# Cached rope keys turned on VectorE and moved by DMA; the last stage without GpSimd

## The reference

```python
# 8 sequences x 4 new tokens, 8 heads; 64 pages of 128 keys each
def mla_scores(q_lat, q_rope, c_kv, k_rope):        # latent part 256 wide, rope part 64 wide
    s = (einsum('bqhc,bkc->bhqk', q_lat, c_kv) + einsum('bqhr,bkr->bhqk', q_rope, k_rope))
    return s * ATTN_SCALE
...
def step(carry, pages):                              # running maximum, sum and accumulator
    m, l, acc = carry
    ck = cache_ckv[pages]
    kr = cache_krope[pages]
    s = mla_scores(q_lat, q_rope, ck, kr)
    m_new = jnp.maximum(m, jnp.max(s, axis=-1))
    alpha = jnp.exp(m - m_new)
    p = jnp.exp(s - m_new[..., None])
    l = l * alpha + jnp.sum(p, axis=-1)
    acc = acc * alpha[..., None] + einsum('bhqk,bkc->bhqc', p, ck)
    return (m_new, l, acc), None
...
out = ys[pos] * w_sorted                             # two expert rows of a token, by its gates
x = x + sum of the two
y = rmsnorm(x, norm_f_g)
```

## Time and profile before

| | us |
|---|---|
| median of 3 runs | 2081.01 (2080.91 to 2081.49) |
| the profiled execution | 2080.76 |
| its span, first to last instruction | 2078.8 |
| TensorE busy | 1874.1 (90%) |
| VectorE busy | 601.1 (29%) |
| ScalarE busy | 447.6 (22%) |
| GpSimd busy | 282.7 (14%) |
| mean granted TensorE clock | 0.948 |

### The profile page before, as it was taken

The page is one execution under the profiler, slowest core; times in us unless marked ns, Lnnn a source line. Parts: engine busy times, 40 slices in busy tenths (PEclk is TensorE's granted clock), DMA queues, the critical chain, the costliest instruction groups (busy, mean ns, idle before and its releaser), DMA issues. The chain is left out here.

```text
span 2078.8 us, 27133 instructions
## 1 busy us (share of the span) xinstructions
PE 1874.1 (90%) x10842; PEld 1112.7 (54%) x10842; DVE 601.1 (29%) x1358; ACT 447.6 (22%) x938; POOL 282.7 (14%) x424
## 2 busy tenths in 40 slices
PE   7999999999999999988999997999598988888870
PEld 5644444444455656756666664565355555555540
DVE  3110000000003334334555555466322211111116
ACT  3211111100012333232344442222110110110113
POOL 1021111000000000002222220122311111111101
PEclk9999999999999999998999998999698998999985
DMA  8212220222110000006777775444599999999966
GB/s 240 90 71 72 78 72 31 78 77 79 60 48 1 1 1 1 1 0 251 266 282 273 276 279 208 157 182 158 186 399 419 419 417 413 418 402 399 399 247 250
DMA packets 91425, 400.28 MB, mean 193 GB/s; under 512 B 22656, under 2 KB 28256, under 8 KB 60544
## 3 DMA queue, kind: packets, MB, share of 16 engines
q1 hardware_dynamic: 71040, 297.50, 36.6%
q0 software_dynamic: 20160, 101.24, 12.9%
q10 hardware_dynamic: 128, 0.20, 0.0%
HBM read 372.44 MB, written 46.88 MB: 202 GB/s over the span
## 5 line engine op out<-in xcount | busy, mean ns | idle before, releaser
L790 PE MATMUL psum<-arena 128*128 128x512 f32 (+1 forms) x1280 | 527.4, 567 | 0.0
L790 PEld LDWEIGHTS psum<-arena 128*128 128x128 f32 x1280 | 239.6, 190 | 259.8 <-issue 235.8
L1219 PE MATMUL psum<-arena 128*64 128x256 f32 (+1 forms) x2048 | 287.3, 415 | 65.5 <-DMA arena<-in_w_up_dram 65.1
L1219 PEld LDWEIGHTS psum<-arena 128*64 128x64 f32 (+1 forms) x2048 | 204.3, 156 | 138.7 <-issue 84.7
L1831 DVE COPY arena<-psum 128x512 f32<-128x512 f32 (+5 forms) x52 | 27.8, 544 | 522.4 <-PE psum L858 228.1
L1002 PEld LDWEIGHTS psum<-arena 128*128 128x128 f32 x1280 | 142.4, 142 | 29.3 <-issue 26.0
L1002 PE MATMUL psum<-arena 128*128 128x128 f32 x1280 | 154.1, 277 | 2.4 <-DVEq L1879 2.4
L1238 PE MATMUL psum<-arena 128*64 128x512 f32 (+1 forms) x512 | 131.3, 595 | 0.7 <-DVE arena L2145 0.7
L1376 ACT ACTIVATE arena<-psum 128x512 f32<-128x512 f32 (+1 forms) x72 | 40.5, 562 | 411.5 <-PE psum L790 400.7
L1393 ACT COPY arena<-psum 128x512 f32<-128x512 f32 x160 | 90.5, 587 | 176.8 <-PE psum L1002 176.8
L1887 DVE COPY arena<-psum 128x512 f32<-128x512 f32 x160 | 109.8, 691 | 36.6 <-PE psum L1002 34.0
(11 more groups left out here) (296 smaller groups left out, 1925.3 us busy)
## 6 DMA issues: line engine op xcount, KB each, us to landing
arena<-in_w_gate_dram SPq DMA_DIRECT2D x64, 1024.0 KB
arena<-in_w_up_dram SPq DMA_DIRECT2D x64, 1024.0 KB
arena<-in_w_down_dram SPq DMA_DIRECT2D x64, 1024.0 KB, 21.8
arena<-in_w_in_dram SPq DMA_DIRECT2D x8, 2048.0 KB, 7.9
z_act<-arena SPq DMA_DIRECT2D x64, 256.0 KB
arena<-z_act SPq DMA_DIRECT2D x8, 2048.0 KB, 9.7
arena<-in_x_prompt_dram SPq DMA_DIRECT2D x16, 512.0 KB, 4.7
arena<-y_rows SPq DMA_DIRECT2D x8, 1024.0 KB, 9.9
```

Source lines behind the costliest of these rows:

```text
L790: last = mm(out[:, 0:w], xn_t[:, k, t * P:t * P + P], w_blk[n % 2][:, k, 0:w], start=(k == 0), stop=(k == KD - 1))
L1219: last = mm(bank(2 + u)[rows, DE * x:DE * x + DE], xg_t[u][:, k, rows], w_e[slot][x][:, k, :], start=(k == 0), stop=(k == KD - 1))
```

## The change

**Rope part of the cache.** TensorE's units become the eight of the latent part; they use four banks (`u % 4`), and both copying engines have four copies. The rope part goes another way. `rope_blocks` on VectorE turns `kr[q]` in 32x32 blocks, one instruction for each half of the 64 features, into `kr_b[0]` and `kr_b[1]` (128 partitions x 512). After it, partition 32a+f of `kr_b[c]` holds feature 32c+f of the 512 keys in partitions 32a to 32a+31. `rope_move` on SP then issues eight transfers of 32 partitions x 2 KB that put these side by side as 64 partitions x 2048 keys, in one of the two halves of `kr_t2`. `score` reads it by a stepped view: pieces of 32 values.

There is one `kr_b`. `rope_blocks(n+2)` stands in round n of VectorE after its copies and before its sum update, and waits until the moves of chunk n+1 have landed (`rk_in`). The moves of n+2 wait for the blocks (`rk_t`) and for the scores of n (`c_s`). The scores of n+1 wait for the moves of n+1. `x_again(0)`, whose buffer now overlaps `kr_t2`, is issued after the stage's end, ahead of `w_o`.

**Last stage.** Tiles 2, 4 and 6 (`PE_TILES`) are summed by TensorE: `x2` times the identity, plus each expert row times a diagonal of gates (`diag`, made by VectorE), in PSUM; ScalarE and VectorE read the sum there. VectorE scales all nine tiles, two tiles behind the sums. ScalarE's scaling and GpSimd's multiplication are gone.

```diff
         def turned_at(u):
-            kind, j, c = turn_units[u]
-            return ck_t[:, c, j, :] if kind == "c" else kr_tt[:, j, :]
+            j, c = turn_units[u]
+            return ck_t[:, c, j, :]
...
+        def row_sum(t):
+            if t in PE_TILES:
+                return bank(2 * PE_TILES.index(t), 2)
+            return fin[t][0:rows_of(t), :]
...
+            def rope_move(s):
+                for c in range(2):
+                    for a in range(4):
+                        sp.dma_start(kr_t2[DR * s + 32 * c:DR * s + 32 * c + 32, 512 * a:512 * a + 512],
+                                     kr_b[c][32 * a:32 * a + 32, :]).then_inc(rk_in[s], 16)
+
+            for n in range(NCH):
+                sp.wait_ge(rk_t, n + 1)
+                if n >= 2:
+                    sp.wait_ge(c_s, n - 1)
+                rope_move(n % 2)
             for t in range(2):
                 sp.wait_ge(c_pv, NCH - 3 + t)
                 z_load(t)
-            x_again(0)
...
             sp.dma_start(g2, norm2_g[0].partition_broadcast(P)).then_inc(uv_in, 16)
+            x_again(0)
             sp.dma_start(w_o_sb, w_o[0].rearrange("(k p) n -> p k n", p=P)).then_inc(wo_in, 16)
...
-            def score(n):
+            def score(n, s, use):
+                half = slice(DR * s, DR * s + DR)
+                rope = kr_t2[half, :].rearrange("p (a r k) -> p r a k", a=4, r=PG)
                 for e in range(2):
-                    pe.wait_ge(kt_in[e], 5 * n + 5)
+                    pe.wait_ge(kt_in[e], 4 * n + 4)
+                pe.wait_ge(rk_in[s], use)
                 for c in range(3):
                     for j in range(4):
-                        half = slice(DR * (j % 2), DR * (j % 2) + DR)
+                        first = key_row(j, 0)
                         last = mm(bank(5)[RS * j:RS * j + RS, :], q_now[:, c, :] if c < 2 else qr_now[half, :],
-                                  ck_t[:, c, j, :] if c < 2 else kr_tt[half, j // 2, :], start=(c == 0), stop=(c == 2))
+                                  ck_t[:, c, j, :] if c < 2 else rope[:, first:first + 7:2], start=(c == 0), stop=(c == 2))
...
+            pe.wait_ge(moe_end, 1)
+            pe.wait_ge(r_dve, NT + 3)
+            for k, t in enumerate(PE_TILES):
+                pe.wait_ge(f_in[t % 4], 16 * (t // 4 + 1))
+                for half in range(2):
+                    cols = slice(512 * half, 512 * half + 512)
+                    mm(bank(2 * k + half), ident, x2[:, t, cols], start=True, stop=False)
+                    mm(bank(2 * k + half), diag[t][0], y2[t][:, cols], start=False, stop=False)
+                    last = mm(bank(2 * k + half), diag[t][1], y2[t][:, D + 512 * half:D + 512 * half + 512], start=False, stop=True)
+                last.then_inc(r_pe, 1)
...
-            def scale_odd(n):
-                act.wait_ge(f_inv, n + 1)
-                A(fin[n][0:rows_of(n), :], fin[n][0:rows_of(n), :], ACT.Copy, scale=stat8[n][0:rows_of(n), 1:2]).then_inc(f_sc, 1)
-
...
-            for t in range(1, NT, 2):
-                pool.wait_ge(f_sc, t // 2 + 1)
-                G.tensor_tensor(fin[t], fin[t], gf, ALU.mult).then_inc(f_okp, 1)
...
+            def rope_blocks(q, arrived, moved=None):
+                dve.wait_ge(c_in[q % 4], arrived)
+                if moved is not None:
+                    dve.wait_ge(rk_in[(q + 1) % 2], moved)
+                for c in range(2):
+                    last = V.transpose(kr_b[c].rearrange("p (r k) -> p r k", r=PG), kr[q % 4][:, :, 32 * c:32 * c + 32])
+                last.then_inc(rk_t, 1)
+
+            rope_blocks(0, 32)
             turned(0, range(1, NU, 2))
+            rope_blocks(1, 32, P)
...
                     if more:
                         turned(n + 1, range(1, NU, 2))
+                    if q < 2 or not last_batch:
+                        rope_blocks(q + 2, 32 * i + 32 * ((q + 2) // 4 + 1), 2 * P * i + P * ((q + 1) // 2 + 1))
                     dve.wait_ge(c_p, n + 1)
...
+            dve.wait_ge(moe_end, 1)
+            for t in PE_TILES:
+                for c in range(2):
+                    last = ts(diag[t][c], ident, gates[:, t, c:c + 1], None, ALU.mult)
+            last.then_inc(r_dve, 1)
...
             for t in range(NT):
                 r = rows_of(t)
-                dve.wait_ge(f_in[t % 4], 16 * (t // 4 + 1))
-                step(stt(fin[t][0:r, :], y2[t][0:r, 0:D], gates[0:r, t, 0:1], x2[0:r, t, :], ALU.mult, ALU.add))
-                stt(fin[t][0:r, :], y2[t][0:r, D:2 * D], gates[0:r, t, 1:2], fin[t][0:r, :], ALU.mult, ALU.add).then_inc(f_sum, 1)
-                if t >= 1:
-                    last_scale(t - 1)
+                if t not in PE_TILES:
+                    dve.wait_ge(f_in[t % 4], 16 * (t // 4 + 1))
+                    step(stt(fin[t][0:r, :], y2[t][0:r, 0:D], gates[0:r, t, 0:1], x2[0:r, t, :], ALU.mult, ALU.add))
+                    stt(fin[t][0:r, :], y2[t][0:r, D:2 * D], gates[0:r, t, 1:2], fin[t][0:r, :], ALU.mult, ALU.add).then_inc(f_sum, 1)
+                if t >= 2:
+                    last_scale(t - 2)
+            last_scale(NT - 2)
             last_scale(NT - 1)
```

77 lines of the change are left out of this document (36 added, 41 removed).

## The result

| | before | after |
|---|---|---|
| median of 4 runs, us | 2080.96 (2075.41 to 2081.49) | 2157.86 (2150.04 to 2163.55) |
| ratio to before | | 1.0373 (95%: 1.0333 to 1.0413) |
| the profiled execution, us | 2080.76 | 2163.55 |
| its mean granted TensorE clock | 0.948 | 0.934 |

A forecast was written before the change was run, and what follows sets the result against it. The prediction took TensorE to bound the cache stage before the change, and rope moves delayed by the gather after it: 2080.8 + 6.1 (start) - 0.9 (first round) + 17.1 (other rounds) - 10.3 (last stage) = 2093 us, range 2041 to 2108.

The forecast's parts named there:

- The chain: Cache stage: weighing releases the next gather, which delays the next moves and so the scores; round 10.1 us, +17.1 us.
- L: Cache stage: the time when a chunk's rope keys land; the next was put at L-d+11.6 us.
- d: Cache stage: how long TensorE's scores wait for the rope keys to land; forecast 1.5 us a round.
- They end when gather and moves are through: Cache stage: the moves lie inside the gather and land after 6.7 us of gather, 1.3 of moves, 0.5 of signal.
- The turn between queues: DMA engines, cache stage: gather and move packets alternate one against one, so moves last about as long as a gather's 16 packets.
- the first rival: Cache stage: moves hidden, landing at 6.5 us, loop 8.0 us under TensorE's 8.63; total 2044 us, chance 0.30 (2040 to 2060).
- the first round: Cache stage: its first round still has free engines and takes 8.63 us, -0.9 us.
- Issues: SP's queue, cache stage: eight transfers issue in 3.41 us, 0.43 each; in quiet the last lands 5.1 us after the first issue.
- The third: Rival, cache stage: transfers start 2 us later under load or transposes take 1.38; 15 us per us; 2108, no separate chance.
- The start: Start of the cache stage: first moves join four queued gathers and land at 975.8 us; +6.1 us, bounds 0 and +6.1.
- The last stage: Last stage: TensorE sums three tiles and VectorE ends at 2061.8 instead of GpSimd at 2072.16; -10.3 us, bounds -5 and -11.3.

The follow-up runs named there:

- e_fill: The changed kernel with 20 useless TensorE transposes a round before the scores' wait for the rope keys: 2148.6 us, ratio to before 1.0350.
- e_gather8k: The changed kernel with each latent gather of 16 KB rows issued as two gathers of 8 KB rows, same bytes: 2164.6 us, ratio to before 1.0420.
- e_queues: The changed kernel with four of a chunk's eight moves issued on ScalarE's queue instead of SP's: 2156.7 us, ratio to before 1.0390.
- e_two_first: The changed kernel with two pairs of block buffers, block transposes moved to the round's end, rope rows gathered before latent rows: 2129.2 us, ratio to before 1.0252.
- e_nogather: The changed kernel with the gathers inside the loop over sequences cut to 16 bytes a row: 2048.2 us, ratio to before 0.9864.

## Why the prediction was wrong

**The chain was right, one term of it was too small.** The prediction had L' = L - d + 3.1 + X, with X = 8.5 from the gather's reaching the engines to the landing (6.7 of gather, 1.3 of moves, 0.5 of signal), and a round of 8.63 + d. In the trace, the weighing starts at 1087.57 and 1096.75, so L - d is 1089.3 and 1098.5, and the landings are 1103.54 and 1113.53: X = 11.1 and 11.9. With X = 11.5 the same two equations give d = 3.0 and a round of 11.6 us; e_fill, whose clock stays up, has 11.73. The failed step is the size of X, the sentence "They end when gather and moves are through" with its 6.7 + 1.3 + 0.5 us. In the long rounds the sentence itself holds, and its terms are too small: the engines are full for 10.7 us instead of 8.0, some 7.7 of this gather where 6.7 stood, 2.0 of the moves where 1.3 stood, and 1.0 of the gather after, which had begun before the moves were through. In the short rounds the moves do not share the engines with the gather's 16 KB rows at all: they are served behind them, in 4.4 us where 1.3 stood. From the last packet to the landing it is 0.9 and 0.7 us; no row had shown the 0.5. That is 46 us of the miss (31 x 1.5).

**The turn between queues was half right.** From the earlier trace rows I took "one against one, whatever their size". Where both queues are served it is so, 46 packets beside 42 in the changed kernel and 95 beside 86 in e_gather8k. What the prediction did not have is the stretch before, in which queued moves are not served at all: 3.4 us and 67 rows of 16 KB in the long round shown, 3.0 us and 105 rows of 8 KB in e_gather8k, 1.6 us one pair of rounds later (1116.5 to 1118.1), and in the short round shown until the gather's rows are through. What decides between these is open. The Trainium skill, "DMA: Bandwidth & Descriptors", section on queues, rings and completion order, says that an engine changes rings only behind a whole packet, and that such a packet has 9 to 17 descriptors as a rule. The prediction took its packet for a record of the trace. Turns of 9 to 17 records are not what the trace shows where both queues are served: there the 47 records of moves stand singly between the gather's. A row packet's length, on which the first rival rested (cut to 4096 bytes, the moves would be hidden), brought no gain in either run that cut it.

**The clock was no term of the sum.** I priced a wait of TensorE at its length. One of 5 us also costs up to 2.5 us in what follows (scores busy for 5.38 us instead of 2.9 in 1127 to 1133.5). The busy time grew by 41 us; part of it replaced idle time. What it costs net is, by the profiled executions, the 0.5 us a round of e_fill, 12.24 - 11.73, 31 x 0.5 = 16 us. By the medians' ratios it is 0.0023 of 2081, 5 us, with overlapping intervals, so this term is the least certain one. The last 5 us of the rounds' miss are 4 that e_fill stands above 11.6 and 1.5 of the first round, which was not shorter. The warning was in the earlier trace rows, granted clock 0.77 in the stretch ahead of the rounds, which has a short wait, against 1.00 in them; I used the low level for the last stage alone.

**Issues.** Eight took 5.1 us, not 3.4, and without a gather the last packet starts 6.2 us after the first issue, where 5.1 stood for the landing; e_queues shows that in the real queue this cost next to nothing.

**The rivals.** The first (moves hidden, 2044 us) stood on 8.0 us of DMA time a round. The moves alone take 2.1 of it, not 1.3, and with the gather's 6.7 that is 8.8, a little over TensorE's 8.63; mixed, the two took 9.4 a round in the changed kernel (0.77 x 12.24) and 10.6 in e_two_first. Whether another order comes nearer to 2044 is not shown. The third had the right direction (each us on L is half a us a round) and the wrong source: the transposes took 1.31 us for the pair, as forecast.

**The start**: +11.0 us instead of +6.1. Moves landed at 978.0, not 975.8, and the scores behind 9.71 us of idle time took 5.50 us, 2.6 over the price used.

**The last stage**: -12.9 us instead of -10.3, from two errors of opposite sign (and the forecast's own waits add up to 2061.6, not 2061.8). I counted six matmuls a tile; there are twelve instructions (an fp32 product is two), and the first tile takes 7.8 us, its first half at the low clock (two instructions 2.05 us, later 1.02), so VectorE waits 2.96 us and ends 36.7 us after the first load, not 35.0. But I took the same end behind it, 6.6 us, and it is 2.4: before, GpSimd's last product belonged to a full tile of 512 KB, now the last store is the ninth tile's 128 KB. 1.7 - 4.2 = -2.5. That the forecast came within 3 us here is in part luck. All scalings are back at 1.28 us, as forecast.

Together, as a sum of the differences above: 4.9 (start) + 67.7 (rounds) + 0.9 (between) - 2.6 (last stage) = 70.9 us above the 2092.8 of the sum, 2163.7; the profiled execution is 2163.55.

## What to carry to other kernels

Small transfers queued beside a gather are held up as if they belonged to it: here they first stood still for up to 3.4 us or until its rows were through, then took turns record by record, and landed 11 to 12 us after the gather had reached the engines. So what hangs on them has to be issued one gather earlier, with buffers and source rows that allow it, and only while the engines' time of both together is below the round. Price a wait of TensorE with the clock that it loses, and add up the DMA time of a round before counting any transfer as hidden. Two edits of one change are worth trying apart: here one of them alone is the gain.

## What the hardware showed that I had not expected

- Useless work made a kernel's rounds shorter: 20 transposes more a round, 2.4 us, and the round went from 12.24 to 11.73 us in the profiled executions, with the granted clock at 1.00 instead of 0.89; the whole time did not change clear of its interval.
- Two queues took turns by single records, 16 KB of a gather against 2 KB of a move (46 packets beside 42 in 2 us), but only after a stretch of 3.4 us in which no queued move was served.
- The granted clock fell behind the wait, not in it: granted 0.98 in 4.7 us without TensorE, 0.63 in the 4.4 us of work after it.
- On-chip moves of 2 KB rows on 32 partitions take 2.1 us of all 16 engines for 512 KB with no gather beside them (e_nogather), about 250 GB/s, where the gather reached 412.
- A VectorE transpose of 128 x 512 values in 32 x 32 blocks takes 0.66 us, about as a copy of that size (0.69).
